# Prompt attention scores: TensorE reads every fourth column of the feature-major queries and keys itself, its tile loop written out

## The chip, the cores and the metric

The kernel runs on one core of one Trainium2 chip. The metric is the device time of one launch in microseconds (us). "PE" is TensorE, "DVE" VectorE, "ACT" ScalarE, "POOL" GpSimd, "SP" SyncE.

## The reference

Two decoder layers over a prompt of 512 positions and 32 sample tokens (8 sequences of 4). Only the second layer's dilated attention matters here:

```python
DIL_PATTERNS = ((128, 1), (512, 4), (2048, 16))        # window, dilation; 8 heads of 64 in each group
def attend(q_blk, rows):                                # steps = arange(n_keys) * dilation
    idx = rows[:, None] - steps[None, :]
    valid = idx >= 0
    kg = jnp.take(k, jnp.maximum(idx, 0), axis=1, mode='clip')
    vg = jnp.take(v, jnp.maximum(idx, 0), axis=1, mode='clip')
    s = jnp.einsum('bqhd,bqkhd->bhqk', q_blk, kg).astype(jnp.float32)
    s = jnp.where(valid[None, None], s + bias, NEG)
    lse = jax.nn.logsumexp(s, axis=-1)
    ...
```

The three groups' outputs are added with weights from their logsumexps, and multiplied by the output matrix. Around it stand, in each layer, a half-step SwiGLU network, the mixer, another half-step network, and a layer norm behind each. Everything is float32.

## The kernel before

All activations lie feature-major: 128 features on the partitions, 544 tokens (512 prompt, 32 sample) along the free dimension. Weights stream in from HBM through two buffers; ACT rounds each to `w_hi`, DVE takes the rest `w_lo`, and PE adds three fp32r products (line 622). That is the bulk of the program. Each engine has a program of its own, written in order by hand, and they meet at semaphores; there is no scheduler.

The attention of the prompt works on four tiles r = 0 to 3. Tile r holds the 128 queries at positions 4q + r, since a dilation of 4 or 16 then only meets keys of the same tile. A tile has 8 turns, one for each head h, and in each PE issues:

- `turn_probs(r, h)`: transposes the exponentials of head h (line 1015), once ACT has made them (line 1342);
- `scores(r, h + 2)`: two heads ahead, crossing into the next tile for h = 6 and 7. For groups 1 and 2 (dilations 4 and 16) it multiplies the tile's 128 queries by its 128 keys (line 917); for group 0 it multiplies each 32 queries by 256 consecutive keys (lines 924 and 927);
- `sample_values`: three products of the sample attention in six of the eight turns (line 992);
- `values(r, h)`: lines 1025 to 1032.

A product of float32 (not fp32r) is issued as two instructions, each with a weight load (LDWEIGHTS) of its own, so line 917 runs 4 times in a head and lines 924 and 927 10 times. At a tile's end come `sample_outputs` (line 1004) and the turn of the tile's outputs (line 1055), for which PE waits on DVE.

The queries `qt` (12 chunks of 128 features, 544 tokens) and keys `kt12` (8 chunks, 512 tokens) have tile r in every fourth column, 16 bytes apart. DVE gathers them into `q_r` and `k_r` with adjacent columns: `qk_tile(r, c)` makes five copies of 128x128 (lines 1666 and 1668) and raises `qk_ok`, on which PE's `scores` waits. The tile 0 copies stand ahead of the sample softmax in DVE's program; those of tile r + 1 follow heads 1, 3, 5 and 7 of tile r. Otherwise DVE's turn is `head(r, h)`: add the biases (lines 1728 and 1729), take the maximum (1731) and negate it (1733), for ACT's exponentials. At a tile's end DVE takes the sample outputs (1710), scales the tile's (1751), and adds the samples' (1718), and only then comes head 0 of the next tile. PE, ACT and DVE have tile 0 and tile 3 written out and tiles 1 and 2 in a loop. Group 0 reads its keys from `kt0` with adjacent columns.

Of the kernel before, what the change touches and what calls it, by code (L numbers as in the profile page):

```python
# [30 lines left out]
P = 128  # L31
D, SEQ, DEC_B, DEC_S = 1024, 512, 8, 4
# [11 lines left out]
GC = GW // P  # L44
NG = 3
# [4 lines left out]
QB = SEQ // P  # L50
# [21 lines left out]
FIRST, AFTER = {}, {}  # L72
# [84 lines left out]
def build(nc, A, O):  # L157
# [3 lines left out]
    def sb(where, name, shape, dt=F32):  # L161
        return where.enter_context(nc.sbuf_tensor("t_" + name, shape, dt))

    def sem(name):
        return ctx.enter_context(nc.semaphore(name))

    with ctx:
# [72 lines left out]
        qt = sb(rh, "q_feat", [P, NG * GC, T])  # L240
        hq = ExitStack()
# [11 lines left out]
        hq.close()  # L253

        ot = sb(hq, "o_feat", [P, GC, T])
        q_r = sb(hq, "q_tile", [P, NG * GC, P])
        k_r = sb(hq, "k_tile", [P, 2 * GC, P])
        v_p = [sb(hq, "v_prompt0", [P, QB, GW])]
        b12 = sb(hq, "bias12", [P, HEADS, 256])
        sb(hq, "not_used", [P, 3 * P])  # L260
        kt12 = sb(hq, "k_feat12", [P, 2 * GC, SEQ])
# [48 lines left out]
        w_used = [sem(f"w_used{s}") for s in range(2)]  # L310
# [91 lines left out]
        kt_in = sem("kt_in")  # L402
        v_in = sem("v_in")
        b12_in = sem("b12_in")
        b0_pad = sem("b0_pad")
        qk_ok = sem("qk_ok")
        s_done = sem("s_done")
        s_ok = sem("s_ok")
        p_ok = sem("p_ok")
# [203 lines left out]
        def _(pe):  # L613
# [291 lines left out]

            def scores(r, h, first):
                c, lo = h // 2, DH * (h % 2)
                out = pa[:, h % 2, :]  # L910
                hd = slice(lo, lo + DH)
                if h % 2 == 0:
                    pe.wait_ge(qk_ok, GC * r + c + 1)
                if h >= 2 or not first:
                    pe.wait_ge(s_ok, HEADS * r + h - 1)
                for g in (1, 2):
                    nc.tensor.matmul(out[:, (g + 1) * P:(g + 2) * P], q_r[hd, g * GC + c, :],  # L917
                                     k_r[hd, (g - 1) * GC + c, :], start=True, stop=True)
                for b in range(QB):
                    q = q_r[hd, c, 32 * b:32 * b + 32]  # L920
                    rows_ = slice(32 * b, 32 * b + 32)
                    if b == 0:
                        for half in range(2):
                            nc.tensor.matmul(out[rows_, half * P:(half + 1) * P], q, kt0[hd, c, 0:P],  # L924
                                             start=True, stop=True)
                    else:
                        m = nc.tensor.matmul(out[rows_, 0:256], q, kt0[hd, c, (b - 1) * P:(b + 1) * P],
                                             start=True, stop=True)
                m.then_inc(s_done, 1)
# [5 lines left out]
            for g in range(NG):  # L935
                for c in range(GC):
# [4 lines left out]
                                         start=True, stop=True)  # L941
# [115 lines left out]

            pe.wait_ge(snv_ok, 1)
            tile(0, True, False)
            with pe.Fori(1, QB - 1) as r:  # L1060
                tile(r, False, False)
            tile(QB - 1, False, True)
            linear("wo", lambda k: ohi[:, k, :], lambda k: olo[:, k, :],
                   lambda s, i: pe.wait_ge(res_made, DC * RES.index("wo") + 2 * i - 1 + s),
                   each=lambda k: pe.wait_ge(o_ready, k + 1))
# [319 lines left out]
        def _(dve):  # L1385
# [272 lines left out]
                m = nc.vector.memset(b0[0:32, h, 0:P], NEG)  # L1658
            m.then_inc(b0_pad, 1)

            def qk_tile(r, c):

                q = qt[:, :, 0:SEQ].rearrange("p (g c) (q r) -> p g c q r", g=NG, r=QB)
                k = kt12[:].rearrange("p (g c) (q r) -> p g c q r", g=2, r=QB)
                for g in range(NG):
                    nc.vector.tensor_copy(q_r[:, g * GC + c, :], q[:, g, c, :, r])
                for g in range(2):
                    m = nc.vector.tensor_copy(k_r[:, g * GC + c, :], k[:, g, c, :, r])
                m.then_inc(qk_ok, 1)

            dve.wait_ge(kt_in, 32)
            for s in range(2):
                dve.wait_ge(w_used[s], FIRST["wo"])
            for c in range(GC):
                qk_tile(0, c)


            dve.wait_ge(srow_t, 1)
            dve.wait_ge(sb_evac, 1)
            for k in range(2):  # L1680
# [55 lines left out]
            def tile(r, last):  # L1736
                for h in range(HEADS):
                    head(r, h)
                    if h % 2 and not last:
                        qk_tile(r + 1, h // 2)  # L1740
                if last:
                    round_lo("wo", 0, 0)
                    round_lo("wo", 1, 0)
                dve.wait_ge(p_ok, HEADS * (r + 1))
                step.add(nc.vector.reciprocal(a_stat[:, 3, r, :], a_stat[:, 2, r, :]))
                dve.wait_ge(dve_step, step.value())
                sample_values(r)
                dve.wait_ge(pv_done, HEADS * (r + 1))
                if not first_turn(r):
                    dve.wait_ge(on_t, r)  # L1750
                nc.vector.tensor_tensor(o_n[:].rearrange("p (h d) -> p h d", d=DH),
                                        pc[:, 0, :].rearrange("p (h d) -> p h d", d=DH),
                                        a_stat[:, 3, r, :].unsqueeze(2).to_broadcast([P, HEADS, DH]), ALU.mult) \
                    .then_inc(on_ok, 1)
                sample_outputs(r)
# [174 lines left out]
```

## Time and profile before

| | us |
|---|---|
| median of 3 runs | 2411.59 |
| lowest and highest | 2408.76, 2417.56 |
| the profiled execution, own time | 2412.17 |
| its span, first to last instruction | 2410.5 |

The times below are from the span's start. The prompt's attention lies between about 1727 and 1934 us. The profile lists each engine's instructions with their start, their length, and what ended the engine's idle time before them. The granted TensorE clock is printed as a share of full speed: 1.0 is 2.4 GHz, 0.5 is 1.2 GHz. Ends of matmuls are modelled, so starts are the safer reading.

### The profile page before, as it was taken

To read this page: it belongs to the slowest core of one execution; us is meant where nothing else is said; L and a number is where in the kernel's file an instruction comes from. 1 tells how busy PE (TensorE), PEld (TensorE's weight loads), DVE (VectorE), ACT (ScalarE), POOL (GpSimd) and SP (SyncE) were. 2 spreads that over 40 slices of the span, in tenths; PEclk is the share of its full clock that TensorE was granted. 3 is DMA by queue.
4 is the path that set the end of the run, shared out by engine and by line. 5 is a ranking of instruction groups with operands and counts; after the bars stand their busy time and mean duration, and the time that the engine had idled before them with its cause. 6 is when DMAs were issued, how large, how long until landed. Compare 5 with 4: busy or idle time off the path is not lost.

```text
span 2410.5 us, 42104 instructions
## 1 busy us (share of the span) xinstructions
PE 2256.6 (94%) x17383; PEld 2149.2 (89%) x17383; DVE 923.2 (38%) x1178; ACT 672.2 (28%) x937; POOL 265.6 (11%) x246
## 2 busy tenths in 40 slices
PE   7999999787999999799999979999899979999997
PEld 7999999787999999799999979998744469999996
DVE  3233332676333323433333242377333363333224
ACT  2222221333322222232222132222222252222222
POOL 0000022105000002200000220210101050000122
PEclk8999999899999999899999989999889989999998
DMA  4233332122222232242223232576734212232321
GB/s 129 79 119 120 104 90 88 45 73 70 70 87 87 87 102 84 59 150 86 87 87 98 85 132 79 184 253 194 242 126 134 66 58 83 87 88 87 101 85 49
DMA packets 376316, 248.90 MB, mean 103 GB/s; under 512 B 7862, under 2 KB 360478, under 8 KB 375694
## 3 DMA queue, kind: packets, MB, share of 16 engines
q1 hardware_dynamic: 366151, 209.99, 29.4%
q0 software_dynamic: 10096, 37.94, 4.5%
q8 instruction: 49, 0.80, 0.1%
q14 instruction: 20, 0.16, 0.0%
HBM read 230.63 MB, written 22.35 MB: 105 GB/s over the span
## 4 chain that ended last, share of the span: by engine, by line
PE 85%; DVE 6%; DMA 4%; issue 2%; ACT 2%; SPq 1%; POOL 1%; DVEq 0%; ACTq 0%; POOLq 0%
PE pair L622 72%; PE pair L642 3%; PE pair L992 3%; DMA t_w_raw<-in_attn_w_kv 3%; DVE t_stream L1504 1%; PE pair L917 1%; PE pair L759 1%; DVE t_work L1506 1%; PE pair L1015 1%; PE pair L1025 1%; ACT t_w_hi L1098 1%; DVE t_u_sum L1546 1%; PE pair L924 1%; DVE t_w_lo L1394 0%; PE pair L1032 0%
## 5 line engine op out<-in xcount | busy, mean ns | idle before, releaser
L1394 DVE TENSOR_TENSOR t_w_lo<-t_w_raw,t_w_hi 128x1024 fp32r<-128x1024 f32 (+2 forms) x302 | 421.9, 1397 | 774.0 <-ACT t_w_hi L1098 773.9
L622 PE MATMUL pair<-t_x_hi,t_w_hi 128*128 128x272 f32 x2944 | 615.2, 291 | 12.4 <-DVE t_w_lo L1394 9.9
L622 PE MATMUL pair<-t_x_lo,t_w_hi 128*128 128x272 f32 x2944 | 610.4, 288 | 0.0
L622 PE MATMUL pair<-t_x_hi,t_w_lo 128*128 128x272 f32 x2944 | 609.4, 288 | 0.0
L1098 ACT ACTIVATE t_w_hi<-t_w_raw 128x1024 fp32r<-128x1024 f32 (+2 forms) x302 | 336.2, 1113 | 912.6 <-PE pair L622 854.3
L622 PEld LDWEIGHTS pair<-t_x_hi,t_w_hi 128*128 128x128 f32 x2944 | 462.5, 189 | 14.6 <-ACT t_elementwise L1145 6.4
L622 PEld LDWEIGHTS pair<-t_x_lo,t_w_hi 128*128 128x128 f32 x2944 | 467.9, 190 | 0.0
L622 PEld LDWEIGHTS pair<-t_x_hi,t_w_lo 128*128 128x128 f32 x2944 | 462.6, 189 | 0.0
L622 PE MATMUL pair<-t_h_hi,t_w_hi 128*128 128x272 f32 x1408 | 292.2, 289 | 0.0
L622 PE MATMUL pair<-t_h_lo,t_w_hi 128*128 128x272 f32 x1408 | 290.3, 287 | 0.0
L622 PE MATMUL pair<-t_h_hi,t_w_lo 128*128 128x272 f32 x1408 | 290.0, 287 | 0.0
L1793 POOL TENSOR_TENSOR t_work<-t_work,t_stream 128x544 f32<-128x544 f32 x42 | 59.1, 1407 | 1542.9 <-DVE t_stream L1480 1541.3
L622 PEld LDWEIGHTS pair<-t_h_lo,t_w_hi 128*128 128x128 f32 x1408 | 222.1, 188 | 0.0
L622 PEld LDWEIGHTS pair<-t_h_hi,t_w_lo 128*128 128x128 f32 x1408 | 219.7, 188 | 0.0
L622 PEld LDWEIGHTS pair<-t_h_hi,t_w_hi 128*128 128x128 f32 x1408 | 219.7, 188 | 0.0
L1461 DVE TENSOR_TENSOR t_elementwise<-t_elementwise,pair 128x544 f32<-128x544 f32 x88 | 63.5, 721 | 271.3 <-PE pair L622 270.5
L1145 ACT ACTIVATE t_elementwise<-pair 128x544 f32<-128x544 f32 x88 | 55.0, 625 | 381.5 <-PE pair L622 381.5
L1480 DVE SCALAR_TENSOR_TENSOR t_stream<-pair,t_stream 128x544 f32 (+1 forms) x48 | 34.8, 725 | 218.6 <-PE pair L622 218.6
L642 PE MATMUL pair<-t_x_hi,t_w_hi 128*128 128x272 f32 x192 | 45.5, 322 | 68.8 <-DVE t_x_lo L1519 63.0
L1795 POOL TENSOR_TENSOR t_work<-t_work,t_elementwise 128x544 f32<-128x544 f32 x42 | 102.7, 2445 | 0.0
L642 PEld LDWEIGHTS pair<-t_x_hi,t_w_hi 128*128 128x128 f32 x192 | 34.9, 218 | 70.9 <-issue 70.9
L622 PE MATMUL pair<-t_kv_in_hi,t_w_hi 128*128 128x272 f32 x384 | 82.4, 296 | 0.0
(222 smaller groups left out, 2173.6 us busy)
## 6 DMA issues: line engine op xcount, KB each, us to landing
t_w_raw<-in_ffn_w SPq DMA_DIRECT2D x176, 512.0 KB, 3.8
t_w_raw<-in_ffn_w SPq DMA_DIRECT2D x64, 704.0 KB, 4.5
t_cached<-in_cache_kv_w POOLq DMA_DIRECT2D x16, 1024.0 KB, 8.6
t_cached_v<-in_cache_kv_w POOLq DMA_DIRECT2D x16, 1024.0 KB, 7.8
t_w_raw<-in_attn_w_kv SPq DMA_DIRECT2D x24, 512.0 KB, 7.2
t_w_raw<-in_attn_w_q SPq DMA_DIRECT2D x12, 512.0 KB, 3.9
scratch_bias_rows<-scratch_bias_row SPq DMA_DIRECT2D x12, 384.0 KB
t_w_raw<-in_pool_w_in SPq DMA_DIRECT2D x8, 512.0 KB, 3.7
```

Source lines behind the costliest of these rows:

```text
L622: m = nc.tensor.matmul(out[:, j, 0:HALF], w[:, at + k, :], a(k)[:, j * HALF:(j + 1) * HALF], start=first and k == 0 and n == 0, stop=last ...
L642: m = nc.tensor.matmul(ps[s][:, j, 0:HALF], w[:, k, :], a[:, k, j * HALF:(j + 1) * HALF], start=k == 0 and n == 0, stop=k == DC - 1 and n ...
L759: m = nc.tensor.matmul(out[:, j, 0:HALF], invd[:], a[:, j * HALF:(j + 1) * HALF], start=first, stop=not first)
L917: nc.tensor.matmul(out[:, (g + 1) * P:(g + 2) * P], q_r[hd, g * GC + c, :], k_r[hd, (g - 1) * GC + c, :], start=True, stop=True)
L992: m = nc.tensor.matmul(pd[32 * s:32 * s + 32, 0, :], p_b[s][:, t, :], v_c0[s][:] if t == 0 else v_c[s][:, t - 1, :], start=t == 0, stop=t ...
L1098: nc.scalar.activation(whi[s][:, 0:KT[stage], :], raw[s][:, 0:KT[stage], :], ACT.Copy) \
L1145: nc.scalar.activation(split(sg[:]), halves(pa), ACT.Silu).then_inc(gate_silu, 1)
L1394: nc.vector.tensor_tensor(wlo[s][:, 0:k, :], raw[s][:, 0:k, :], whi[s][:, 0:k, :].bitcast(F32), ALU.subtract).then_inc(lo_made[s], 1)
L1461: nc.vector.tensor_tensor(split(hf[:]), split(sg[:]), halves(pb), ALU.mult).then_inc(h_made, 1)
L1480: nc.vector.scalar_tensor_tensor(out=split(x[:, c, :]), in0=halves(out), scalar=scale, in1=split(x[:, c, :]), op0=ALU.mult, op1=ALU.add) \
L1793: nc.gpsimd.tensor_tensor(accs[:], accs[:], x[:, c, :], ALU.add).then_inc(acc_made, 1)
L1795: nc.gpsimd.tensor_tensor(accq[:], accq[:], sq[:], ALU.add).then_inc(acc_made, 1)
```

## The change

`scores` takes its operands directly from `qt` and `kt12`, by a view of every fourth column. Of groups 1 and 2 both the weights (queries) and the moving columns (keys) are read that way; of group 0 only the weights, 32 at a time. The wait on `qk_ok`, the semaphore, `qk_tile` and all of its calls go, and with them DVE's waits on the keys and on the weight buffers ahead of tile 0. PE's loop over tiles 1 and 2 is written out. A placeholder keeps the other buffers where they were.

```diff
-        q_r = sb(hq, "q_tile", [P, NG * GC, P])
-        k_r = sb(hq, "k_tile", [P, 2 * GC, P])
+        sb(hq, "not_used_before", [P, NG * GC * P + 2 * GC * P])
...
+            def every_fourth(t, part, c, r):
+                return t[part, c, 0:SEQ].rearrange("p (q r) -> p q r", r=QB)[:, :, r]
+
             def scores(r, h, first):
...
-                if h % 2 == 0:
-                    pe.wait_ge(qk_ok, GC * r + c + 1)
...
                 for g in (1, 2):
-                    nc.tensor.matmul(out[:, (g + 1) * P:(g + 2) * P], q_r[hd, g * GC + c, :],
-                                     k_r[hd, (g - 1) * GC + c, :], start=True, stop=True)
+                    nc.tensor.matmul(out[:, (g + 1) * P:(g + 2) * P], every_fourth(qt, hd, g * GC + c, r),
+                                     every_fourth(kt12, hd, (g - 1) * GC + c, r), start=True, stop=True)
                 for b in range(QB):
-                    q = q_r[hd, c, 32 * b:32 * b + 32]
+                    q = every_fourth(qt, hd, c, r)[:, 32 * b:32 * b + 32]
...
             tile(0, True, False)
-            with pe.Fori(1, QB - 1) as r:
-                tile(r, False, False)
-            tile(QB - 1, False, True)
+            for r in range(1, QB):
+                tile(r, False, r == QB - 1)
...
-            def qk_tile(r, c):
-
-                q = qt[:, :, 0:SEQ].rearrange("p (g c) (q r) -> p g c q r", g=NG, r=QB)
-                k = kt12[:].rearrange("p (g c) (q r) -> p g c q r", g=2, r=QB)
-                for g in range(NG):
-                    nc.vector.tensor_copy(q_r[:, g * GC + c, :], q[:, g, c, :, r])
-                for g in range(2):
-                    m = nc.vector.tensor_copy(k_r[:, g * GC + c, :], k[:, g, c, :, r])
-                m.then_inc(qk_ok, 1)
-
-            dve.wait_ge(kt_in, 32)
-            for s in range(2):
-                dve.wait_ge(w_used[s], FIRST["wo"])
-            for c in range(GC):
-                qk_tile(0, c)
...
                     head(r, h)
-                    if h % 2 and not last:
-                        qk_tile(r + 1, h // 2)
```

On PE, at the passage from tile 0 into tile 1, before (names are output<-moving,weights or the two operands; the ISA and REGISTER_ALU rows are the loop's register work):

```order
2254 L1055 MATMUL pair<-t_ident,t_o_tok 128x128 x4
2255 L1060 UNCONDITIONAL_BRANCH
2256 L1060 ISA
2257 L1013 REGISTER_ALU
2258 L1015 MATMUL pair<-t_ident,t_p_prompt 128x128 x4
2259 L913 ISA
2260 L917 MATMUL pair<-t_k_tile,t_q_tile 128x128 x2
2261 L924 MATMUL pair<-t_k_feat,t_q_tile 32x128 x2
2262 L927 MATMUL pair<-t_k_feat,t_q_tile 32x256 x3
```

and with the change, where line numbers are one to three lower:

```order
2254 L1054 MATMUL pair<-t_ident,t_o_tok 128x128 x4
2255 L1014 MATMUL pair<-t_ident,t_p_prompt 128x128 x4
2256 L916 MATMUL pair<-t_k_feat,t_q_feat 128x128 x2
2257 L923 MATMUL pair<-t_k_feat,t_q_feat 32x128 x2
2258 L926 MATMUL pair<-t_k_feat,t_q_feat 32x256 x3
```

The matmuls are the same in number and order; the branch and the register work are gone, and the operands are the undivided tensors.

On DVE, ahead of the sample softmax and at heads 1 and 2 of tile 0, before:

```order
480 L1658 MEMSET t_bias 32x128 x8
481 L1666 COPY t_q_tile<-t_q_feat 128x128 x3
482 L1668 COPY t_k_tile<-t_k_feat 128x128 x2
...
489 L1681 TENSOR_TENSOR t_work<-pair,t_samp_bias 128x384
...
505 L1733 TENSOR_SCALAR t_a_stats<-t_a_stats 128x1
506 L1666 COPY t_q_tile<-t_q_feat 128x128 x3
507 L1668 COPY t_k_tile<-t_k_feat 128x128 x2
508 L1728 TENSOR_TENSOR t_s_prompt<-pair,t_bias 128x256
```

and with the change:

```order
480 L1656 MEMSET t_bias 32x128 x8
481 L1662 TENSOR_TENSOR t_work<-pair,t_samp_bias 128x384
...
497 L1714 TENSOR_SCALAR t_a_stats<-t_a_stats 128x1
498 L1709 TENSOR_TENSOR t_s_prompt<-pair,t_bias 128x256
```

The 20 copies ahead of tile 0 and the 20 in each of tiles 0, 1 and 2 are gone, and nothing takes their place.

## Rows read from the trace of the kernel before

**Rows 1.** The page: shares of the span, by engine; then the chain that ended last.
```profile
PE 2256.6 (94%) x17383; PEld 2149.2 (89%) x17383; DVE 923.2 (38%) x1178; ACT 672.2 (28%) x937; POOL 265.6 (11%) x246
...
PE 85%; DVE 6%; DMA 4%; issue 2%; ACT 2%; SPq 1%; POOL 1%; DVEq 0%; ACTq 0%; POOLq 0%
```
**Rows 2.** Chain, two full-speed turns of tile 0 (start us, us, what).
```profile
1767.85 0.59 PE pair L1015 x4
1768.44 0.64 PE pair L917 x4
1769.08 0.22 PE pair L924
1769.63 2.71 PE pair L992 x6
1772.35 0.59 PE pair L1025 x4
1773.31 0.59 PE pair L1015 x4
```
**Rows 3.** Chain, tile 1 in the loop, and tile 3 written out: same columns.
```profile
1802.85 0.59 PE pair L1015 x4
...
1808.30 0.59 PE pair L1015 x4
...
1895.28 0.59 PE pair L1015 x4
...
1900.73 0.59 PE pair L1015 x4
```
**Rows 4.** Timeline: a full-speed `scores`, then a half-speed one (start, us, engine, line).
```profile
1773.83 0.71 PE L917 MATMUL pair<-t_k_tile,t_q_tile 64*128 64x128 f32 x4
...
1774.46 0.10 PEld L924 LDWEIGHTS pair<-t_k_feat,t_q_tile 64*32 64x32 f32 x1
...
1775.04 1.04 PE L992 MATMUL pair<-t_cached_v_g,t_work 128*32 128x512 f32 x2
...
1795.24 1.22 PE L917 MATMUL pair<-t_k_tile,t_q_tile 64*128 64x128 f32 x4
```
**Rows 5.** Stages: us, busy time of PE, PEld, DVE, ACT, POOL; granted clock; DMA.
```profile
1744.50:1757.50 13.00, 12.93 (x91) 9.33 (x92) 5.65 (x20) 4.12 (x9) 0.00 (x0) 0.50 0.76 270
1757.50:1794.20 36.70, 33.75 (x251) 16.25 (x247) 12.79 (x38) 8.14 (x16) 5.60 (x16) 0.97 0.34 108
1794.20:1801.90 7.70, 7.70 (x25) 3.14 (x25) 3.23 (x11) 2.11 (x5) 0.00 (x0) 0.56 0.43 164
```
**Rows 6.** Timeline: DVE ahead of tile 0, last column its idle time before.
```profile
1718.97 0.64 DVE L1666 COPY t_q_tile<-t_q_feat 128x128 f32<-128x128 f32 x3 [10.97 <-DMA t_k_feat<-scratch_kt]
...
1722.26 0.46 DVE L1668 COPY t_k_tile<-t_k_feat 128x128 f32<-128x128 f32 x2
...
1725.63 0.56 DVE L1681 TENSOR_TENSOR t_work<-pair,t_samp_bias 128x384 f32<-128x384 f32 x1 [2.92 <-PE pair L953]
```
**Rows 7.** Waits, 1690 to 1935 us: who, for whom, total, times, longest.
```profile
DVE t_s_prompt L1728 <- PE pair L927: 80.9, 24, 6.0
```
**Rows 8.** Timeline: last copies of tile 0, and the passages into tiles 1, 2 and 3.
```profile
1777.31 0.45 DVE L1668 COPY t_k_tile<-t_k_feat 128x128 f32<-128x128 f32 x2
...
1788.81 0.68 DVE L1710 COPY t_work<-pair 64x512 f32<-64x512 f32 x1 [10.89 <-PE pair L992]
...
1794.20 1.11 PE L1015 MATMUL pair<-t_ident,t_p_prompt 128*128 128x128 f32 x4 [2.95 <-ACT t_p_prompt L1342]
...
1837.60 0.42 DVE L1728 TENSOR_TENSOR t_s_prompt<-pair,t_bias 128x256 f32<-128x256 f32 x1 [0.43 <-issue]
...
1886.88 1.11 PE L1015 MATMUL pair<-t_ident,t_p_prompt 128*128 128x128 f32 x4 [2.55 <-ACT t_p_prompt L1342]
```
**Rows 9.** Single lines: durations in ns, min/median/max.
```profile
L1666 DVE COPY t_q_tile<-t_q_feat x48: 260/271/286, 1719.0 to 1875.9; 128x128 f32<-128x128 f32 x24, 128x128 f32 x24
...
L1728 DVE TENSOR_TENSOR t_s_prompt<-pair,t_bias x32: 423/424/425, 1741.9 to 1919.0; 128x256 f32<-128x256 f32 x32
...
L1614 DVE TENSOR_TENSOR t_k_times_q<-pair,t_cached x64: 679/691/693, 1548.8 to 1690.3; 128x512 f32<-128x512 f32 x64
```
**Rows 10.** The same for ACT: adjacent writes, then 16 bytes apart.
```profile
L1335 ACT ACTIVATE t_elementwise<-pair x2: 362/370/377, 1734.7 to 1735.5; 128x256 f32<-128x256 f32 x1, 32x256 f32<-32x256 f32 x1
...
L1349 ACT ACTIVATE t_pt_prompt<-pair x32: 576/597/598, 1745.9 to 1926.2; 128x512 f32<-128x512 f32 x32
...
L1362 ACT ACTIVATE t_o_feat<-pair x4: 1066/1078/1087, 1791.3 to 1931.2; 128x512 f32<-128x512 f32 x2, 128x512 f32 x2
```

More of the change, by code:

```diff
@@ L405, in build @@
         b0_pad = sem("b0_pad")
-        qk_ok = sem("qk_ok")
         s_done = sem("s_done")
```

## The prediction

> **What bounds the kernel now.** I read the page first: PE is busy for 94% of the span, and 85% of the chain that ended last is PE [rows 1]. An average says nothing of the stretch that is changed, so the next view is that chain between 1727 and 1934 us. In the middle of a tile it is PE alone, one matmul behind the other: transposes, scores, sample products, values, and from one turn to the next 1773.31 - 1767.85 = 5.46 us [rows 2]. DVE waits there: its line 1728 stood for 80.9 us in all on PE's scores, in 24 of 32 heads [rows 7]. So PE decides, and anything that DVE saves inside a tile is slack on top of slack. The reader is to see two things: what DVE loses was not on the path, and every nanosecond that a scores matmul grows is.
>
> At the passages between tiles PE stands still for some 3 us, for ACT's exponentials, which wait for DVE's line 1733, which waits for DVE's work at the end of the tile [rows 8]. Behind each of them the clock is low: the stage of the first turn of tile 1 has 0.56, the first three turns of tile 0 0.50, and the rest of tile 0 0.97 [rows 5]. This matters for counting: of 32 scores, five of tile 0 (two ahead of it, three in its first turns) and the one in the first turn of each later tile run near 1.2 GHz, 8 in all, and 24 run at 2.4 GHz.
>
> **Part 1, the 80 copies go.** Each is 271 ns long [rows 9]; starts in a row of three are (0.64 - 0.27)/2 = 0.18 us apart [rows 6], so a group of five takes about 0.9 us and all sixteen groups some 15 us of DVE. What of that lay on the path?
> The four groups ahead of tile 0 ran from 1718.97 to 1722.72, and DVE then waited 2.92 us for PE's line 953 [rows 6]. PE itself was held there by another chain. Worth 0.
> The groups inside a tile stand between DVE heads that wait for PE [rows 7]. Worth 0.
> The last group of a tile, which could delay the passage, ended in tile 0 at 1777.76, and DVE idled 10.89 us after it before the tile's end work [rows 8]. Worth 0.
> What may be left is the sequencer of DVE: into tile 2 line 1728 started 0.43 us after its engine was free, put down to issue, and DVE keeps its own loop [rows 8]. If fewer register instructions shorten that, it is at most 0.43 us once. I take 0.
> PE's wait on `qk_ok` was met long before in each case, and goes at no gain. Nothing is queued behind a new wait, since none is added.
>
> **Part 2, PE's loop is written out.** Compare a turn in the loop with one outside it: 1808.30 - 1802.85 = 5.45 in tile 1, 1900.73 - 1895.28 = 5.45 in tile 3 [rows 3], 5.46 in tile 0 [rows 2]. The register work of the loop is hidden behind the matmuls. At the passages it lies in a wait for ACT that is 2.95 us in the loop and 2.55 us outside [rows 8], so its absence is worth 0 too; the 0.4 us between these two is DVE's, above. The written-out tile is more code to fetch; tiles 0 and 3 are such code already, and run at the same pace. I take 0 and keep +1 us for the range.
>
> **Part 3, the strided reads.** This is the one term that can move the time. Per head 4 instructions of line 917 read 128 weights and 128 moving columns that now stand 16 bytes apart, and 10 of lines 924 and 927 load 32 such weights, with their moving columns still adjacent. All of it is on the path. At 2.4 GHz a scores takes 1775.04 - 1773.83 = 1.21 us, 0.63 of them before the first of line 924 [rows 4]. Four instructions in 0.63 us are at most 0.16 us for 128 columns, 1.23 ns a column with the start of the group in it. A float32 instruction of 512 columns, line 992, takes 2.71/6 = 0.452 us [rows 2], or 0.88 ns a column. That is the demand to be met: a new 16-byte place every 0.88 ns at full clock, and every 1.77 ns at half clock.
> No row shows PE reading this way. The nearest rows disagree.
> Below: DVE's copies read exactly these operands at this stride. Would it show if that were slow? Adjacent operands of 256 and 512 elements took 424 and 691 ns, that is 1.04 ns an element and 157 ns beside, which makes 290 ns for 128. The strided copy took 271 [rows 9]. So a strided read goes at one element in 1.04 ns or better, with no sign of a penalty. If PE could do no better than that, each of the 24 x 4 fast instructions of line 917 would grow by 128 x (1.04 - 0.88) = 20 ns, 2.0 us in all.
> Above: ACT's write of 512 elements 16 bytes apart took 1078 ns where adjacent ones took 597 [rows 10]. Adjacent: (597 - 370)/256 = 0.89 ns an element, so 1.83 ns at the stride. If PE's reads had that rate, line 917 would grow by 24 x 4 x 128 x (1.83 - 0.88) = 11.7 us at full clock and by 8 x 4 x 128 x (1.83 - 1.77) = 0.2 us at half. The weight loads of 32 add 24 x 10 x 32 x 0.95 = 7.3 us if nothing hides them, and little if they hide behind the moving columns of the other three quarters of the array. Together 12 to 19 us.
> I take the value of the DVE row, because it is a read of the same tensors, where ACT's is a write; and because PE takes a float32 column at half the rate of its clock, so that it asks for little more than DVE gets. The term is then 0 to 2 us; I take 0.5.
>
> The Trainium skill speaks against the change here: "Advanced Engine Details and Errata", section "SBUF Cachelines", says that SBUF has lines of 16 bytes, that two hits on a line are needed to absorb the access latency, and that a new line at each access costs a penalty, whose size it does not give. At this stride each element is a line of its own. The DVE rows show no penalty at 1.04 ns an element; no row shows PE at 0.88. By that rule the sum would be the first rival's.
>
> **Sum.** The profiled execution's own time 2412.17, minus 0, plus 0, plus 0.5: 2412.7. It lies 0.6 above the median of the runs shown, so the forecast for a median is about 2412.
>
> **The rivals.** First, slower: PE's reads at 16 bytes apart go at the rate of ACT's writes. The mechanism is a wait for each new place in memory, in both streams of line 917, 128 instructions. It decides as soon as the time for a place is above 0.88 ns; 12 us (0.5%) are reached between 1.5 ns (weight loads in the open) and 1.9 ns (hidden). For it: the ACT rows, and that line 917 is the only place in the kernel where PE would read so fast with such gaps. Against it: the DVE rows. Price 12 to 19 us, middle 15: 2427.
> Second, worse: weights and moving columns both come at that rate and also share it, since they lie on the same partitions and now each need a place per element. Then a column of line 917 takes 3.66 ns: 24 x 4 x 128 x (3.66 - 0.88) = 34 us at full clock, 8 x 4 x 128 x (3.66 - 1.77) = 8 at half, and the 7 of the small weight loads: 2461. Against it: today both are loaded side by side at full pace, though with four elements to a place.
> Third, faster: the missing DVE work shortens the passages between tiles. The passages stand still for about 3 us each and there are three of them; were all of it gone, it would be 9 us, and the rows let me expect 0.4 at most. To be seen outside a measurement it would need 12 us, for which there is no source in the attention. An unlooked-for cause is left a small chance, at about 2398.
>
> **How the numbers follow.** Forecast, about 2412: 0.62. First rival, 2424 to 2431: 0.29. Second, about 2461: 0.05. Faster: 0.04. Within 0.5% (12 us, about what a measurement of this kernel can tell from no change) are the forecast and the lower edge of the first rival, 0.03 of its 0.29: same 0.65, slower 0.31, faster 0.04. The runs before lay between 2408.8 and 2417.6, so the low end is 2407. The high end has to take in the first rival, 2431. That leaves the second, the faster case and some of the edges out, about 0.1.
>
> **What would show it.** Right: the four instructions of line 916 (917 before) still take about 0.63 us to the first of line 923, a scores 1.21, a full-speed turn 5.45 us; DVE's copies gone and its wait at line 1709 (1728 before) longer by about as much as they took; the passages unchanged at some 3 us. First rival: 1.1 to 1.2 us to line 923, a turn of 5.9 to 6.2 us, half-speed turns hardly changed. Second: over 1.5 us to line 923. Faster: shorter waits of line 1014 for the exponentials. The prediction is wrong if PE cannot fetch a place every 0.88 ns; nothing else in it has weight.

## The result: slower, and the profile after

| | before | after |
|---|---|---|
| median, us | 2413.57 (4 runs) | 2432.45 (4 runs) |
| lowest and highest | 2408.76, 2417.56 | 2430.65, 2433.88 |
| the profiled execution, own time | 2412.17 | 2430.65 |
| its span | 2410.5 | 2427.4 |
| ratio of the times, 95% interval | | 1.0084, 1.0061 to 1.0106 |

The change costs 0.84%, some 19 us. That is more than the 12 us that a measurement of this kernel can tell from no change. It lies 1.4 us above the end of the forecast's range, 2431, and some 20 above the forecast itself, about 2412; it is the first rival's case.

The page of the kernel after, shares of the span by engine, and the chain that ended last:

```profile
PE 2271.7 (94%) x17383; PEld 2159.9 (89%) x17383; DVE 908.2 (37%) x1098; ACT 672.4 (28%) x937; POOL 265.9 (11%) x246
...
PE 84%; DVE 6%; DMA 4%; issue 2%; ACT 2%; SPq 1%; POOL 1%; ACTq 0%; DVEq 0%; POOLq 0%
```

Against [rows 1], DVE lost 80 instructions and 15.0 us, as counted. PE has the same 17383 instructions and 15.1 us more. The span grew by 16.9. The page already says which of the two the time follows.

The chain of the kernel after, two full-speed turns of tile 0 (start us, us, what), to be held against [rows 2]:

```profile
1776.16 0.59 PE pair L1014 x4
1776.75 1.22 PE pair L916 x4
1777.97 0.26 PE pair L923
...
1778.55 2.71 PE pair L991 x6
1781.26 0.59 PE pair L1024 x4
...
1782.22 0.59 PE pair L1014 x4
1782.81 1.23 PE pair L916 x4
1784.04 0.25 PE pair L923
```

One entry has moved: line 916 takes 1.22 to 1.23 us where line 917 took 0.64. The first small product behind it takes 0.25 instead of 0.22. Transposes, sample products and values are where they were (0.59, 2.71, 0.59). A turn is 1782.22 - 1776.16 = 6.06 us instead of 5.46.

The passage from tile 0 to tile 1 and the half-speed turn behind it, timeline of PE (start, us, last column its idle time before):

```profile
1798.82 1.11 PE L1014 MATMUL pair<-t_ident,t_p_prompt 128*128 128x128 f32 x4 [2.88 <-ACT t_p_prompt L1340]
1799.87 1.30 PE L916 MATMUL pair<-t_k_feat,t_q_feat 64*128 64x128 f32 x4
1801.10 0.43 PE L923 MATMUL pair<-t_k_feat,t_q_feat 64*32 64x128 f32 x1
```

The wait for the exponentials is 2.88 us, 2.95 before [rows 8]. At half speed the four instructions of line 916 take 1801.10 - 1799.87 = 1.23 us: **the same time at either clock**. Before it was 0.64 at full speed [rows 2] and, from 1795.24 [rows 4] to the first small product, 1.15 at half speed:

```profile
1796.39 0.42 PE L924 MATMUL pair<-t_k_feat,t_q_tile 64*32 64x128 f32 x1
```

So what holds them in the changed kernel does not run with TensorE's clock.

The two instructions of line 916 by themselves (duration in ns, min/median/max; first and last start):

```profile
L916 PEld LDWEIGHTS pair<-t_k_feat,t_q_feat x128: 304/326/329, 1727.9 to 1936.2; 64*128 64x128 f32 x128
L916 PE MATMUL pair<-t_k_feat,t_q_feat x128: 404/412/600, 1727.9 to 1936.4; 64*128 64x128 f32 x128
```

Before, for line 917:

```profile
L917 PEld LDWEIGHTS pair<-t_k_tile,t_q_tile x128: 182/188/335, 1727.1 to 1917.9; 64*128 64x128 f32 x128
L917 PE MATMUL pair<-t_k_tile,t_q_tile x128: 272/272/579, 1727.1 to 1918.0; 64*128 64x128 f32 x128
```

Both medians grew by some 140 ns (412 - 272 and 326 - 188) for 128 columns. The smallest weight load, 304, is above the median of before, so none of them escaped.

**Where the 16.9 us of span are.** 24 turns at full speed are 0.61 longer, 14.6 us; 8 scores at half speed are 1.23 - 1.15 = 0.08 longer, 0.6 us; together 15.3. The rest goes with the clock, which came back later in this execution: in each tile the six sample products of the turn in which it comes back took 3.9 to 5.1 us before and 5.1 to 5.3 after, 3.3 more in four tiles. That makes 18.6 where 16.9 are to be explained; the difference of 1.7 was not followed further. How long the clock stays low varies in the runs below from one execution to the next.

DVE waits the more, as it should where it is not the bound:

```profile
DVE t_s_prompt L1709 <- PE pair L926: 104.6, 24, 7.0
```

80.9 us in [rows 7]: its work shrank, PE's turn grew, and both went into the same slack.

### The profile page after: what moved, and what is told of

Its sections match the earlier page's. It is cut to its first block, busy times and chain, and to the rows that moved or that the text cites. A ratio compares the mean times of both kernels' runs of the same rounds, so it can differ in the third digit from the quotient of the medians.

```text
span 2427.4 us, 41903 instructions
## 1 busy us (share of the span) xinstructions
PE 2271.7 (94%) x17383; PEld 2159.9 (89%) x17383; DVE 908.2 (37%) x1098; ACT 672.4 (28%) x937; POOL 265.9 (11%) x246
## 4 chain that ended last, share of the span: by engine, by line
PE 84%; DVE 6%; DMA 4%; issue 2%; ACT 2%; SPq 1%; POOL 1%; ACTq 0%; DVEq 0%; POOLq 0%
PE pair L620 71%; PE pair L640 3%; DMA t_w_raw<-in_attn_w_kv 3%; PE pair L991 3%; PE pair L916 2%; DVE t_stream L1502 1%; PE pair L757 1%; DVE t_work L1504 1%; PE pair L1014 1%; PE pair L1024 1%; ACT t_w_hi L1096 1%; DVE t_u_sum L1544 1%; PE pair L923 0%; DMA t_bias<-scratch_bias_rows 0%; DVE t_w_lo L1392 0%
## 5 line engine op out<-in xcount | busy, mean ns | idle before, releaser
L1096 ACT ACTIVATE t_w_hi<-t_w_raw 128x1024 fp32r<-128x1024 f32 (+2 forms) x302 | 336.2, 1113 | 912.4 <-PE pair L620 854.0
L620 PEld LDWEIGHTS pair<-t_x_hi,t_w_hi 128*128 128x128 f32 x2944 | 462.8, 189 | 14.6 <-ACT t_elementwise L1143 6.4
```

Source lines behind the costliest of these rows:

```text
L620: m = nc.tensor.matmul(out[:, j, 0:HALF], w[:, at + k, :], a(k)[:, j * HALF:(j + 1) * HALF], start=first and k == 0 and n == 0, stop=last ...
L1096: nc.scalar.activation(whi[s][:, 0:KT[stage], :], raw[s][:, 0:KT[stage], :], ACT.Copy) \
```

## The experiments

Two theories stood at first: the strided reads hold PE (with the question which of the two streams, and whether they share a limit), or the time comes from the loop written out or from the missing copies on DVE. Kernels of one group below ran on one chip and share its runs of before.

### First group: the change taken apart

`e1_unroll_only`: before, with PE's loop written out, and nothing else.

```diff
-            with pe.Fori(1, QB - 1) as r:
-                tile(r, False, False)
-            tile(QB - 1, False, True)
+            for r in range(1, QB):
+                tile(r, False, r == QB - 1)
```

> The kernel before with PE's loop over tiles 1 and 2 written out, and nothing else: DVE's copies, their semaphore and the adjacent reads stay. Theory (the strided reads alone cost the time): ratio 1.000, a full-speed turn 5.45 us, four instructions of line 917 in 0.63 us. Rival (the longer program on PE costs): ratio above 1.002, with idle time on PE in tile 1 or 2 put down to issue.

Measured: 2413.97 against 2412.04, ratio 1.0008 (0.9999 to 1.0018, 10 and 13 runs). No difference that can be told.

`e2_strided_copies_kept`: after, with `qk_tile` and its calls put back on DVE, unread by PE.

```diff
+            for c in range(GC):
+                qk_tile(0, c)
...
                     head(r, h)
+                    if h % 2 and not last:
+                        qk_tile(r + 1, h // 2)
```

> The changed kernel with DVE's 80 copies left in; nobody reads their result and PE does not wait for them. Theory (DVE's work lies off the path): the time of the changed kernel, ratio 1.008 to the kernel before, line 917 in 1.23 us. Rival (the copies' absence saved or cost something): a time 1 us or more away from the changed kernel's, at a passage between tiles.

Measured: 2431.13, ratio 1.0085 (1.0069 to 1.0102), the same as after to within the interval, some 4 us either way. The profile is sharper: PE's waits at the three passages are 2.88, 3.37 and 2.55 us in both. Fifteen us of DVE work put back cost nothing that shows, so taking them away had gained nothing, and Part 1 of the sum is 0. Against `e1_unroll_only`, from which this kernel differs in the strided reads and the wait on `qk_ok` alone, the distance is 2431.13 - 2413.97 = 17.2 us: the reads alone cost the time.

`e3_weights_strided` and `e4_moving_strided`: the loop written out and the copies kept, and only one of the two operands of line 917 read from the undivided tensor; in the first also the 32-column weights.

```diff
# e3_weights_strided, against after
-                                     every_fourth(kt12, hd, (g - 1) * GC + c, r), start=True, stop=True)
+                                     k_r[hd, (g - 1) * GC + c, :], start=True, stop=True)
# e4_moving_strided, against before
-                                     k_r[hd, (g - 1) * GC + c, :], start=True, stop=True)
+                                     every_fourth(kt12, hd, (g - 1) * GC + c, r), start=True, stop=True)
```

> Only the queries, which are the weights of lines 917, 924 and 927, are read 16 bytes apart; keys come from DVE's adjacent copies. Loop written out. Theory A (each stream has its own limit, both about 1.9 ns for a place, and they run side by side): the weight loads alone already set the pace, line 917 takes 1.2 us for four and the ratio is about 1.008. Theory B (the two strided streams share one limit, so each alone runs free): line 917 stays near 0.63 us and the ratio within 0.002 of 1. In between: the two add, 0.9 us, ratio 1.004.

> Only the keys, which are the moving columns of line 917, are read 16 bytes apart; queries come from DVE's adjacent copies. Loop written out. Theory A (own limit for each stream, side by side): line 917 takes 1.2 us for four, ratio about 1.007, lines 924 and 927 as before. Theory B (shared limit): 0.63 us, ratio within 0.002 of 1. In between: the two add, 0.9 us, ratio 1.004.

Measured: 2425.25, ratio 1.0058 (1.0041 to 1.0074), and 2425.08, ratio 1.0057 (1.0040 to 1.0074). Either operand alone costs 13 us; both cost 19. Timeline of a full-speed turn, first with strided weights, then with strided moving columns:

```profile
1780.66 0.66 PE L1018 MATMUL pair<-t_ident,t_p_prompt 128*128 128x128 f32 x4
1781.25 1.20 PE L920 MATMUL pair<-t_k_tile,t_q_feat 64*128 64x128 f32 x4
1782.37 0.32 PE L927 MATMUL pair<-t_k_feat,t_q_feat 64*32 64x128 f32 x1
...
1786.63 0.66 PE L1018 MATMUL pair<-t_ident,t_p_prompt 128*128 128x128 f32 x4
```

```profile
1780.76 0.65 PE L1018 MATMUL pair<-t_ident,t_p_prompt 128*128 128x128 f32 x4
1781.35 1.15 PE L920 MATMUL pair<-t_k_feat,t_q_tile 64*128 64x128 f32 x4
1782.43 0.29 PE L927 MATMUL pair<-t_k_feat,t_q_tile 64*32 64x128 f32 x1
...
1786.66 0.66 PE L1018 MATMUL pair<-t_ident,t_p_prompt 128*128 128x128 f32 x4
```

From start to start, the four instructions take 1.12 us with strided weights, 1.08 with strided keys, 1.23 with both, 0.64 with neither (0.63 by the timeline). The excesses 0.49, 0.45 and 0.60 don't add up. The two streams run side by side, each with a limit of its own, and do not share one: with both strided, four instructions take 1.23 us where the second rival's 3.66 ns a column would need 4 x 128 x 3.66 = 1.87. `m1_strides` below shows the same in a longer row. Each lone excess is four streams of about 0.12 us, and both together five of them. That fits a group of four in which the first weight load stands open and the others run beside the products: four loads in the first case, four products in the second, one load and four products with both. This counting is read from the three sums; the rows of `m1_strides` below bear on it.

### Second group: the price of a place, and what hides it

`e5_small_weights_strided`: before, with the loop written out and only the 32-column weights of lines 924 and 927 read from `qt`.

```diff
-                    q = q_r[hd, c, 32 * b:32 * b + 32]
+                    q = every_fourth(qt, hd, c, r)[:, 32 * b:32 * b + 32]
```

> Only the ten weight loads of 32 queries in lines 924 and 927 read 16 bytes apart; line 917 keeps both adjacent copies. Loop written out. Theory (they hide behind the moving columns of the other three quarters of the array): scores grows by under 0.05 us, ratio at most 1.002. Rival (they lie in the open): 0.3 us a head, 7 us, ratio 1.003.

Measured: 2414.11 against 2413.46, ratio 1.0008 (0.9998 to 1.0017, 10 and 19 runs). The load takes 0.13 us instead of 0.10 and hides. The first rival's 7.3 us for small loads in the open don't occur: the first of them shows by 0.03 us a head, under 1 us in all.

`m1_strides`: before, with a tail of measured instructions behind the kernel's own work; its time as a kernel says nothing. Products repeated with columns s apart, and copies of 512 elements on ACT and DVE that read or write s apart. `every(t, s, n)` is the first n columns s apart. Lines 1098 to 1102 have adjacent weights and moving columns 1, 2, 3, 4, 8 apart; 1103 to 1106 have adjacent moving columns and weights 2, 3, 4, 8 apart; 1107 to 1109 have both 2, 4, 8 apart; 1110 to 1113 have 512 moving columns 1, 2, 4, 8 apart; 1114 to 1123 have fp32r operands. One line of each kind:

```diff
+            for _ in range(16): mm = nc.tensor.matmul(pb[:, 1, 0:128], every(x, 1, 128), every(x, 4, 128), start=True, stop=True)
...
+            for _ in range(16): mm = nc.tensor.matmul(pb[:, 1, 0:512], every(x, 1, 128), every(x, 4, 512), start=True, stop=True)
...
+            for w in range(4): m = nc.scalar.activation(work[:, 512 * w:512 * w + 512], every(x, 4, 512), ACT.Copy)
...
+            for w in range(4): m = nc.vector.tensor_copy(work[:, 512 * w:512 * w + 512], every(x, 4, 512))
```

> The kernel before with a measuring tail: after the last transposes PE runs 100 products of 512 columns to bring the clock up and then rows of 16 equal products each, into an unused bank, with weights and moving columns 1, 2, 3, 4 or 8 elements apart, in float32 and float32r; then ACT and DVE copy 512 elements with reads 1, 2, 4 and 8 apart and writes 2 and 4 apart. The time of the kernel means nothing, the starts within each row do. Theory (a place of 16 bytes is the unit): 2 apart is free, 4 and 8 apart cost the same, for float32 about 1.8 ns a column against 0.88 with adjacent columns; float32r pays more in proportion, since it asks twice as fast. Rival (a fixed price for each separate element, whatever the distance): 2 apart costs as much as 4. Rival for DVE: its reads 4 apart are as fast as adjacent ones. For ACT, the forecast took the writes' price for the reads': expected now, reads 4 apart at the same 1.8 ns as writes.

Float32 on PE (ns, min/median/max; first and last start). The time for one instruction is the distance of the starts by 31:

```profile
L1098 PE MATMUL pair<-t_stream x32: 272/275/275, 2490.7 to 2494.2; 128*128 128x128 f32 x32
...
L1099 PE MATMUL pair<-t_stream x32: 273/275/280, 2494.3 to 2497.8; 128*128 128x128 f32 x32
...
L1100 PE MATMUL pair<-t_stream x32: 332/344/344, 2498.0 to 2503.3; 128*128 128x128 f32 x32
...
L1101 PE MATMUL pair<-t_stream x32: 398/405/405, 2503.5 to 2510.5; 128*128 128x128 f32 x32
...
L1102 PE MATMUL pair<-t_stream x32: 410/412/413, 2510.7 to 2518.0; 128*128 128x128 f32 x32
...
L1105 PEld LDWEIGHTS pair<-t_stream x32: 317/330/330, 2527.4 to 2534.6; 128*128 128x128 f32 x32
...
L1108 PE MATMUL pair<-t_stream x32: 415/416/489, 2546.4 to 2553.7; 128*128 128x128 f32 x32
...
L1112 PE MATMUL pair<-t_stream x32: 1057/1079/1079, 2589.8 to 2617.7; 128*128 128x512 f32 x32
```

Moving columns adjacent: 3.5/31 = 0.113 us for 128, 0.88 ns a column. 2 apart (8 bytes): the same. 3 apart: 0.171, 1.34 ns. 4 apart (16 bytes): 0.226, 1.76 ns. 8 apart: 0.235, 1.84 ns. Weights 4 apart: 7.2/31 = 0.232, 1.81 ns. Weights and columns both 4 apart: 7.3/31 = 0.235, no more than either alone. With 512 columns 4 apart: 27.9/31 = 0.90 us, 1.76 ns. So **a new place of 16 bytes costs PE about 1.8 ns for each float32 stream**. The five distances fit this one price: columns 2 apart share a place by twos and need one every 1.76 ns anyway, so they are free; 3 apart need three places for four columns, and pay 3/4 of it.

The rows also bear on the counting in the group of four. In a long row an instruction takes 0.113 us with adjacent operands and 0.235 with both strided, so four take 0.45 and 0.94. The group in the attention takes 0.63 and 1.23, that is 0.18 and 0.29 more. The difference, 0.11 us, is what one strided weight load costs beyond an adjacent one.

The other engines, copies of 512 with the read adjacent and then 16 bytes apart:

```profile
L1424 ACT ACTIVATE t_work<-t_stream x4: 614/614/631, 2690.4 to 2691.9; 128x512 f32<-128x512 f32 x4
...
L1430 ACT ACTIVATE t_work<-t_stream x4: 1090/1092/1107, 2694.9 to 2697.9; 128x512 f32<-128x512 f32 x4
```

```profile
L1838 DVE COPY t_work<-t_stream x4: 421/421/427, 2709.4 to 2710.4; 128x512 f32<-128x512 f32 x4
...
L1844 DVE COPY t_work<-t_stream x4: 609/610/618, 2712.3 to 2713.9; 128x512 f32<-128x512 f32 x4
```

ACT: 478 ns more for 512, whether it reads or writes that way (its strided write, line 1439, took 1103, which agrees with 1078 in [rows 10]). DVE: 189 ns more, so its own strided copies do pay.

### The passages

If the strides cost a fixed amount in each head, the other place where PE loses time can be worked on apart. The last cause of each passage's wait is DVE's head 0 of the next tile, which stands behind the tile's end work.

`p1_head_first`: before, with head 0 of the next tile ahead of that work on DVE, and its exponentials ahead of the last `turned` on ACT.

```diff
# ACT
-                exps(r, 0, first)
...
+                    elif not (isinstance(r, int) and r == QB - 1):
+                        exps(r + 1, 0, False)
                     turned(r, h, first)
...
+            exps(0, 0, True)
# DVE
-                for h in range(HEADS):
+                for h in range(1, HEADS):
...
+                if not last:
+                    head(r + 1, 0)
...
+            head(0, 0)
```

> The kernel before, with adjacent copies and its loop, but DVE takes head 0 of tile r + 1 ahead of the end of tile r, and ACT its exponentials ahead of turning head 7, so that PE finds them at once at the passage. It tells what the clock does when PE no longer stands still there. Theory (the low clock behind each passage comes from PE's 3 us of idle time): the three waits of line 1015 fall from 2.9 us to under 1, the clock stays at full speed there, and each passage gives back 3 us of waiting and 3 to 5 us of half speed: 2390 to 2395 us. Rival (the low clock has another cause, or the wait is replaced by the one for DVE's scaled outputs): 2403 to 2412.

`p2_head_first_strided`: the same two edits made on after.

> The same reordering on the changed kernel, with its strided reads. If the low clock hid a part of the strided reads' price (at half speed they cost 0.08 us a head and at full speed 0.60), then with fewer heads at half speed the distance to the reordered kernel with adjacent copies grows from 18 us to about 20. Rival (part of the 18 us was the clock returning later in the changed kernel): the distance shrinks to 15 or 16.

Measured: 2403.12, ratio 0.9954 (0.9938 to 0.9971), and 2416.91, ratio 1.0010 (1.0000 to 1.0019). In `p1_head_first` PE's waits for the exponentials fell from 12.3 us in four to one of 4.3, ahead of tile 0, and those of line 1025 rose from 2.1 to 4.2. The forecast for it, 2390 to 2395 us, missed: a new wait of 1.06 us for ACT stands at two of the three passages, and the clock still falls at these two; only at the first does it stay up.

The price of the strided reads in this surrounding is 2416.91 - 2403.12 = 13.8 us, less than either 20 or 15 to 16, and it does not decide between them. Between the ends of the two intervals it is anything from 7 to 20 us, and the two kernels differ in more than the reads: with its longer scores `p2_head_first_strided` has gaps of only 0.35 us at these two passages, and in its profiled execution the clock is low behind the passages for 6.8 us, where it was 17.1 in that of `p1_head_first`.

### Third group: the distance again, and a kernel that beats both

`e7_after_again` and `e7_unroll_again` are the kernel after and `e1_unroll_only` unchanged, beside each other on one chip in five rounds. `p1_again` is `p1_head_first`. `p3_turn_then_exp` is that kernel with ACT's last two steps of a tile exchanged:

```diff
                     if h + 1 < HEADS:
                         exps(r, h + 1, first)
-                    elif not (isinstance(r, int) and r == QB - 1):
-                        exps(r + 1, 0, False)
                     turned(r, h, first)
+                if not (isinstance(r, int) and r == QB - 1):
+                    exps(r + 1, 0, False)
```

> The changed kernel once more, on one chip with the written-out kernel that reads adjacent copies. Full-speed heads pay 0.6 us each in the traces, 24 of them 14.5, and half-speed heads 0.08 each, together 15.1 us. Theory (nothing but the longer reads): a distance of 15 us to that kernel. Rival (something beside them, such as a clock that returns later): 18 us, as the runs on different chips had it.

> The kernel with PE's loop written out, adjacent copies and DVE's work as before: the partner of the run beside it. Ratio to the kernel before between 1.000 and 1.001.

> The first reordering once more, on one chip with the second: about 2403 us, ratio 0.995 to 0.997.

> The reordered kernel with adjacent copies, where ACT turns head 7 first and then makes the exponentials of the next tile's head 0. In the first reordering PE still waited 1.06 us for ACT at a passage, since the exponentials stood ahead of the turn. Theory: that wait goes, 3 us in all, and with less idle time the clock drops less often: 2396 to 2400 us. Rival (the end of the tile waits for DVE or ACT elsewhere): 2403.

| | median, us | runs | ratio to before, 95% |
|---|---|---|---|
| before | 2412.49 | 18 | |
| e7_after_again | 2430.34 | 6 | 1.0069, 1.0051 to 1.0087 |
| e7_unroll_again | 2412.81 | 12 | 0.9999, 0.9990 to 1.0009 |
| p1_again | 2403.24 | 7 | 0.9951, 0.9931 to 0.9970 |
| p3_turn_then_exp | 2395.31 | 6 | 0.9924, 0.9907 to 0.9940 |

The distance between the kernels that differ in the strided reads and DVE's copies alone is 17.5 us. That is nearer to the rival's 18 than to the 15 of the theory, but between the ends of the two intervals it is 10 to 23, which holds both. In their two profiled executions the spans differ by 17.3 us: 1.3 of it stand ahead of the first scores already (1727.23 against 1725.96 us), and 16.0 lie between these and the turn of tile 3's outputs, with stretches of low clock that add up to about the same. PE's waits at the passages are the same in both, 2.88, 3.36 and 2.55 us. So within the attention this pair gives 16.0 against the 15.3 that the turns explain, with the clock as good as equal. The other 2 us are of the size by which executions of one kernel differ; whether a later return of the clock belongs to the strided reads stays open.

PE's waits in `p3_turn_then_exp` (from 1740 to 1935 us: who, for whom, total, times, longest), and the stages of the same kernel and of `p1_head_first` (us; busy time of PE, PEld, DVE, ACT, POOL; granted clock; DMA):

```profile
PE pair L1015 <- ACT t_p_prompt L1342: 3.6, 1, 3.6
...
PE pair L1025 <- ACT t_pt_prompt L1349: 2.0, 2, 1.4
```

```profile
1790.00:1835.00 45.00, 45.00 (x369) 24.21 (x368) 22.76 (x72) 14.68 (x29) 7.53 (x23) 1.00 0.53 179
1835.00:1890.00 55.00, 55.00 (x461) 29.45 (x461) 22.86 (x66) 16.50 (x34) 5.60 (x16) 1.00 0.30 103
```

```profile
1790.00:1835.00 45.00, 43.94 (x368) 25.48 (x368) 20.54 (x62) 12.17 (x26) 8.38 (x24) 0.95 0.53 179
1835.00:1890.00 55.00, 53.94 (x399) 27.71 (x398) 22.57 (x68) 15.92 (x32) 5.59 (x16) 0.88 0.30 103
```

In `p3_turn_then_exp` PE is busy without a gap through all three passages (about 1790, 1830 and 1875 us), and the clock stays at 1.00; in `p1_head_first` it stands still for 1.06 us in each of the two stretches and the clock falls in both. The gap of `p1_head_first` at the passage from tile 1 to 2, timeline of PE:

```profile
1830.52 0.87 PE L1025 MATMUL pair<-t_v_prompt,t_pt_prompt 128*128 x4 [1.06 <-ACT t_pt_prompt L1349]
```

The exchange lets ACT evacuate the last transposes first, which PE needs at once. It gives 2403.24 - 2395.31 = 8 us, with intervals that just touch. In the profiled execution of `p1_again` the two gaps are 1.06 and 1.05 us and the clock is low behind the passages for 13.7 us; a PE that is busy at half clock loses half of that, so an estimate from these two is 2.1 + 6.8 = 8.9 us. The kernel `p3_turn_then_exp` is 17 us faster than before and 35 faster than after.

Whether a short gap by itself makes the clock fall is not shown. It fell behind each gap of 1.06 us in the two profiled executions with that order, and behind none of the passages without a gap. In `p2_head_first_strided`, with 0.35 us at two passages, it stayed up behind the first (1.00 from 1825 to 1876 us) and fell behind the second.

## Why the prediction was wrong, point by point

**What bounds the kernel: right.** PE alone decides inside a turn, and all that a scores matmul grew is in the end: 0.60 us more in the group, 0.60 more from turn to turn. The count of 24 scores at full clock and 8 at half is what makes 15.3 us come out.

**Parts 1 and 2, worth 0: right**, and now shown by runs, the copies by `e2_strided_copies_kept`, the loop by `e1_unroll_only` and its repetition. The passages kept their waits as well: 2.95, 3.44 and 2.55 us before, 2.88, 3.37 and 2.55 after. The 0.07 at each of the first two comes with PE's loop, since `e7_unroll_again` has 2.88 and 3.36.

**Part 3, the strided reads, put at 0 to 2 us and taken as 0.5: wrong, and the only step that failed.** The term measured 15.3 us by the turns and 17 to 19 by the medians. The two bounds were right to be written down, and the truth lay at the upper one: 1.76 to 1.81 ns a place against 1.83 from the ACT rows [rows 10]. What failed was the choice between them, and both reasons given for it.
The first reason, "a read of the same tensors, where ACT's is a write": the runs show that ACT's reads 16 bytes apart cost what its writes do (1092 and 1103 ns). Direction was no ground to prefer a row.
The second reason, "it asks for little more than DVE gets", took DVE's rate for one that PE would have too. It is DVE's own: 0.37 ns an element of penalty (189/512), on 0.65 adjacent, makes 1.02, while PE gets a place only every 1.8 ns and ACT no faster, from the same kind of tensor.
Under both lies a faulty reading of [rows 9]. The strided copy (271 ns for 128) was held against operations with two operands, adjacent, 1.04 ns an element, and "no sign of a penalty" was concluded. A copy of adjacent elements goes at 0.65 ns. The penalty was there, and it was just large enough to lift the copy to the pace of a slower operation. ACT's pair in [rows 10] was the clean one as to the stride: the same function and width, on an engine whose adjacent pace, 0.89 ns, is PE's 0.88.

**The first rival: right in mechanism, in place and nearly in size.** Expected were 1.1 to 1.2 us to the small products, a turn of 5.9 to 6.2, half-speed turns hardly changed; measured 1.23, 6.06, and 0.08 more. Its lower price, 12 us with the small loads hidden, is short of 15.3 because line 917 was priced as 128 columns an instruction, 0.49 us a head, where 0.60 were measured; by the counting above the rest is the first weight load of each head, which stands open. Its upper price, with the small loads in the open, does not occur. That its middle, 15, fits so well is luck: it lay between two prices neither of which is what happened. The rule of the Trainium skill that was weighed ("Advanced Engine Details and Errata", section "SBUF Cachelines") came out as it says for PE's float32 columns: two hits in a line of 16 bytes cost nothing extra (0.88 ns at 8 bytes), one hit costs double. The size, which it does not give, is 1.8 ns. For fp32r columns two hits were not enough, as the last section shows.

**The second rival, a shared limit:** excluded by the four instructions in 1.23 us and by 0.235 us an instruction in `m1_strides` with both operands strided. **The faster one:** there is no gain in the change, but the passages it pointed to are worth 17 us to an edit that is made for them.

## What to carry to other kernels

Gathering columns on an engine with slack cost nothing here; reading them 16 bytes apart on the engine that decides costs time in every column, 1.8 ns against 0.88 for float32 on PE at full clock. At half clock it was nearly free (1.23 against 1.15 us for the group), and at 8 bytes apart float32 paid nothing. To judge a strided access that the trace lacks, take a pair of rows that differ in the stride alone (same operation, same engine, adjacent and strided), and ask how near that engine's adjacent pace is to the one you price; a strided row held against another operation says nothing. Look at the waits at a passage as well before saving work inside a turn: moving one head of DVE and one step of ACT gave 17 us, where 15 us less work on DVE gave nothing.

## What the runs showed of the hardware that was not expected

**fp32r columns don't follow the float32 price.** In `m1_strides`, 512 adjacent fp32r columns at full clock (timeline; the instructions between the two start at 2667.73, 2667.96 and 2668.18), and then 2, 4 and 8 apart:

```profile
2667.50 0.84 PE L1120 MATMUL pair<-t_x_hi 128*128 128x512 f32 x3
...
2668.41 0.39 PE L1120 MATMUL pair<-t_x_hi 128*128 128x512 f32 x1
```

```profile
L1121 PE MATMUL pair<-t_x_hi x16: 615/630/637, 2668.6 to 2675.4; 128*128 128x512 f32 x16
...
L1122 PE MATMUL pair<-t_x_hi x16: 639/642/643, 2675.9 to 2682.8; 128*128 128x512 f32 x16
...
L1123 PE MATMUL pair<-t_x_hi x16: 607/607/612, 2683.2 to 2689.7; 128*128 128x512 f32 x16
```

Adjacent: (2668.41 - 2667.50)/4 = 0.23 us, 0.44 ns a column. Strided, by the starts, 6.8/15 = 0.453, 0.46 and 0.433 us: 0.85 to 0.90 ns a column at all three distances. So fp32r pays double already at 8 bytes apart, where float32 pays nothing, and at 16 bytes it pays half of float32's price. One price for a place cannot give both. This stays open.

**The clock fell under a PE that never stood still.** Stages of `m1_strides`, columns as above (PE's busy time is the third number, the granted clock the third from the end):

```profile
2640.00:2656.50 16.50, 16.50 (x78) 10.20 (x77) 0.00 (x0) 0.00 (x0) 0.00 (x0) 1.00 0.00 0
2657.00:2666.50 9.50, 9.50 (x35) 8.73 (x36) 0.00 (x0) 0.00 (x0) 0.00 (x0) 0.50 0.01 2
2668.00:2690.00 22.00, 22.00 (x52) 10.23 (x50) 0.00 (x0) 0.00 (x0) 0.00 (x0) 1.00 0.00 0
```

PE is busy for all of 16.5 us at full clock, and then has 0.50 for 9.5 us, in a stretch that begins where the fp32r products load their weights 16 bytes apart (lines 1118 and 1119) and ends in row 1120, whose operands are adjacent. The pace confirms it: the products of row 1120 start every 0.43 us in that stretch and every 0.23 behind it. It happened once in one execution, so it is a thing seen, not one explained.

The low stretches of the attention vary too. Behind the three passages they are 6.8 or 10.2 us each. They add up to 24 us in the profiled execution of before and in those of `e3_weights_strided` and `e4_moving_strided`, 27 in `e1_unroll_only` and in `e7_after_again` and `e7_unroll_again`, and 31 in after and `e2_strided_copies_kept`. With one execution each this neither shows nor excludes a part of the strides in them.

**DVE pays far less for a place than PE and ACT**: elements 16 bytes apart go at about 1.8 ns on PE and 1.95 on ACT by the starts (3.0/3/512), and at 1.0 on DVE. So DVE's pace said nothing of PE's. ACT's did come near it, but that is two engines that agree, not a reason why they should.
